# Feed-forward sums in PSUM banks, another ring placement, meta rows over four column groups, a second attention woven into projections

## What is computed

```python
h = [112 zero rows, 16 meta rows, 256 token rows]                 # first block
proj = rmsnorm(h) @ w_in                                           # q, k, v of 8 heads; q, f, i, g of 4 gated heads
h += concat(stick_breaking(sb_q, sb_k, sb_v), hgrn2(hg_q, hg_f, hg_i) * silu(hg_g)) @ w_out
h += hierarchical_moe(rmsnorm(h))                                  # 32 experts
x = rmsnorm(h[128:])
for layer in (0, 1):                                               # second block
    q, k, v, q_mem = projections of x                              # layer 1: "MoBA", 12 heads of 64, k and v from shared_w_kv
    mix = concat(attention(q, k, v), softmax(q_mem @ km.T / 8) @ vm) @ w_out
    x = layer_norm(ALPHA * x + mix)
    a, b = split(x @ ffn_w_in)                                     # two halves of 2816
    a = causal convolution of a over 3 tokens + bias
    x = layer_norm(ALPHA * x + (gelu(a) * b) @ ffn_w_out)
```

## Time and profile before

| | us |
|---|---|
| median of 3 runs | 1521.02 |
| the profiled execution | 1524.56 |
| its span, first to last instruction | 1522.8 |

### The profile page before, as it was taken

One profiled execution on the slowest core, in us unless ns is written; L12 is line 12 of the kernel. 1 busy time (PEld: TensorE's weight loads), 2 busy tenths in 40 slices (PEclk: granted clock), 3 DMA queues, 4 the chain that ended last, 5 costly groups with the idle time before them and its releaser, 6 DMA issues.

```text
span 1522.8 us, 18334 instructions
## 1 busy us (share of the span) xinstructions
PE 1270.6 (83%) x7464; PEld 821.1 (54%) x7464; DVE 601.2 (39%) x1127; ACT 263.7 (17%) x681; POOL 409.6 (27%) x379
## 2 busy tenths in 40 slices
PE   7999989776656667676998797999979978999995
PEld 6864554322212212122776557999437744999842
DVE  3432424101100000011105624988963052788986
ACT  4313431000000000001124611211001051111100
POOL 4000100000000000000002422988840032598881
PEclk9999889978878877778997899999999999999998
DMA  9613117999999999999633007844335512454300
GB/s 316 209 65 111 56 59 264 381 421 421 422 422 422 422 422 422 422 422 408 235 111 111 1 1 247 279 167 166 138 111 193 166 56 82 161 173 167 139 0 28
DMA packets 112758, 335.72 MB, mean 220 GB/s; under 512 B 6616, under 2 KB 58128, under 8 KB 88109
## 3 DMA queue, kind: packets, MB, share of 16 engines
q1 hardware_dynamic: 110070, 326.33, 56.3%
q0 software_dynamic: 2416, 8.30, 1.6%
q10 hardware_dynamic: 199, 0.06, 0.0%
HBM read 333.59 MB, written 2.86 MB: 221 GB/s over the span
## 4 chain that ended last, share of the span: by engine, by line
PE 62%; DMA 25%; DVE 8%; ACT 3%; issue 2%; SPq 1%; DVEq 0%; ACTq 0%
PE bank L767 23%; DMA ring<-in_w_expert_up 23%; PE bank L1441 18%; PE bank L1489 7%; PE bank L1087 5%; PE bank L1312 1%; DMA ring<-in_a_w_in 1%; PE bank L913 1%; DVE small L2484 1%; PE bank L1361 1%; ACT arena L1870 1%; SPq L664 1%; ACT arena L1879 1%; PE bank L1284 1%; DMA ring<-in_ffn_w_in 1%
## 5 line engine op out<-in xcount | busy, mean ns | idle before, releaser
L1087 PE MATMUL bank<-ring,arena 128*32 128x512 f32 x992 | 152.5, 771 | 122.1 <-DMA ring<-in_w_expert_up 109.6
L767 PE MATMUL bank<-ring,wide_rows 128*128 128x512 f32 (+3 forms) x416 | 172.2, 572 | 1.2 <-DVE wide_rows L2504 1.1
L1087 PEld LDWEIGHTS bank<-ring,arena 128*32 128x32 f32 x992 | 40.6, 137 | 232.8 <-issue 213.9
L767 PE MATMUL bank<-wide_rows,ring 128*128 128x256 f32 (+3 forms) x672 | 152.1, 383 | 4.9 <-DMA ring<-in_a_w_in 2.5
L767 PEld LDWEIGHTS bank<-wide_rows,ring 128*128 128x128 f32 (+1 forms) x672 | 128.0, 198 | 29.4 <-issue 9.3
L2318 DVE TENSOR_TENSOR arena<-arena,bank 64x512 f32<-64x512 f32 x16 | 11.1, 691 | 307.0 <-ACT arena L1764 307.0
L1441 PE MATMUL bank<-R,arena 128*128 128x128 f32 x1056 | 125.1, 275 | 0.0
L767 PEld LDWEIGHTS bank<-ring,wide_rows 128*128 128x128 f32 (+1 forms) x416 | 76.9, 188 | 86.6 <-issue 83.8
L1441 PEld LDWEIGHTS bank<-R,arena 128*128 128x128 f32 x1056 | 121.5, 192 | 0.0
L2772 POOL MEMSET arena<- 128x768 f32 (+2 forms) x3 | 1.1, 412 | 435.2 <-DVE X L2413 435.2
L1441 PE MATMUL bank<-wide_rows,ring 128*128 128x128 f32 x704 | 88.6, 282 | 12.7 <-DMA ring<-in_ffn_w_in 8.5
(11 more groups left out here) (364 smaller groups left out, 1851.8 us busy)
## 6 DMA issues: line engine op xcount, KB each, us to landing
ring<-in_w_expert_down SPq DMA_DIRECT2D x32, 2048.0 KB, 24.1
ring<-in_w_expert_gate SPq DMA_DIRECT2D x31, 2048.0 KB, 19.2
ring<-in_w_expert_up SPq DMA_DIRECT2D x31, 2048.0 KB, 23.7
ring<-in_ffn_w_in SPq DMA_DIRECT2D x44, 1024.0 KB, 8.3
ring<-in_ffn_w_out SPq DMA_DIRECT2D x10, 2048.0 KB, 7.8
ring<-in_w_in SPq DMA_DIRECT2D x7, 2048.0 KB, 15.4
ring<-in_shared_w_kv SPq DMA_DIRECT2D x3, 2048.0 KB, 7.8
ring<-in_w_out SPq DMA_DIRECT2D x2, 2048.0 KB, 10.5
```

Of the source, the lines that this page charges most:

```text
L767: last = pe.matmul(dst, lhsT, rhs, start=k == 0, stop=k == len(pairs) - 1)
L1087: last = pe.matmul(bank[e % 2][at:at + SLOTS, :], xg_tile(e % 2, k)[:, SLOTS * r:SLOTS * r + SLOTS], w[r][:, kk, :], start=k == 0, stop=k ...
```

## The change

**Meta rows.** The meta job now takes 32 stationary columns in place of 16 and sends its eight matmuls to four column groups of the array, two to each (L905); a new job (sbvs, hgis) adds the four partial results with one matmul by a 0/1 matrix by_slice, which GpSimd makes at the start. s0 moves from step 5 to step 6.

**Ring.** From feed-forward 0 on, the load order stays nearly the same (b_in 1 comes first of layer 1), but slots are given by SLOT_ORDER. Unit ffn_in 1 of layer 0 now goes to the slot of cmp_v, in place of that of the memory rows, and ffn_in 4 goes to the latter. b_out 1 goes to the slot of b_in 1, which is read until b_q 2.

**a_in.** Each of its three units is waited for where it is first read.

**Feed-forward.** summed writes its results to the bank y; the taps and the gate read them there; a tile's second bank is free again only after gate. down's products 1 to 7 go to other banks. GpSimd makes the sums of pairs 0 and 1 alone, hidden and weights; VectorE makes those of pairs 2 to 10 alone (pair_summed, in the order of SUM_ORDER). Product 5 of pair 0 waits until after product 6 of pair 1. The last three pairs wait for their sums one by one.

**Layer 1.** The list second_attention gives one order to TensorE and ScalarE, in which projections, attention steps and five eighths of each b_out job ("begun") stand alternately. Units begin with mem. In step i TensorE does scores(i), transposes(i - 2) and values(i - 3). Scores have banks 4 and 5, transposes bank 6 and values bank 7 alone, and so each waits for the unit before it. Outputs go to headT, in R. In feed-forward 1 tile 2's first quarters come ahead of the second token block as well.

The diff, cut to its core:

```diff
...
+SUM_ORDER = list(range(2, LAST_PAIRS[0])) + [STEPS_F - 1, STEPS_F - 3, STEPS_F - 2]
+SLOT_ORDER = (0, 3, 2, 5, 1, 4)
+LATE = 2
...
     ffn(0)
-    order += [("kv", c) for c in range(3)] + [("b_in", c) for c in range(2)] + [("b_out", c) for c in range(2)]
+    order += [("b_in", 1), ("kv", 0), ("b_in", 0), ("kv", 1), ("kv", 2)] + [("b_out", c) for c in range(2)]
     ffn(1)
...
+        placed[i // RING * RING + SLOT_ORDER[i % RING]] = key
...
+def second_attention():
+
+
+    return [("b_qm", 0), ("b_k", 0), ("step", 0), ("b_q", 0), ("step", 1), ("b_v", 0), ("step", 2), ("b_v", 1), ("step", 3), ("step", 4),
+            ("b_k", 1), ("step", 5), ("step", 6), ("b_q", 1), ("step", 7), ("step", 8), ("b_v", 2), ("step", 9), ("b_v", 3), ("step", 10),
+            ("b_k", 2), ("step", 11), ("b_q", 2), ("step", 12), ("begun", 0), ("step", 13), ("begun", 1), ("step", 14), ("begun", 2),
+            ("step", 15), ("begun", 3), ("step", 16), ("step", 17), ("step", 18)]
...
+                for k in range(2):
+                    for r in range(4):
+                        last = pe.matmul(b[SLOTS * r:SLOTS * (r + 1), :], XT[:, 4 * k + r, 0:SLOTS], w[:, 4 * k + r, :],
+                                         start=k == 0, stop=k == 1)
+                last.then_inc(job_done, 1)
+
+            def slices_summed(name, partial):
+                pe.wait_ge(slices_ready, 1)
+                b = to_fill(pe, name)
+                wait_emptied(pe, name[:-1], 2)
+                pe.matmul(b[0:META, :], by_slice[:, :], partial, start=True, stop=True).then_inc(job_done, 1)
...
+                if c not in wa:
+                    wa[c] = wait_weights(pe, ("a_in", c))[:, 0:KT * (A_CUTS[c + 1] - A_CUTS[c])].rearrange("p (k n) -> p k n", k=KT)
...
+                    if layer == 1:
+                        pe.wait_ge(at_tc, u)
...
                     if u >= 4:
                         pe.wait_ge(ph["summed"], u - 3)
                         first_columns(u, 0)
-                        first_columns(u, 1)
...
+                    if u >= 4:
+                        pe.wait_ge(ph["hidden"], u - 3)
+                        first_columns(u, 1)
...
+                    if p == 0:
+                        pe.wait_ge(ph["summed"], FFT - 1)
+                        pe.wait_ge(ph["hidden"], FFT - 3)
                     down(p, 1)
-                    down(p, 2)
-                    pe.wait_ge(ph["h_sums"], p + 1)
+                    pair_summed(p)
                     down(p, 3)
+                    down(p, 4)
+                    down(p, 7)
                     if p == 0:
                         pe.wait_ge(ph["summed"], FFT)
...
+                    if p == 1:
+                        pe.wait_ge(ph["hidden"], FFT - 1)
+                        down(0, 5).then_inc(ph["used"], 1)
+                    if p >= 1:
+                        down(p, 5).then_inc(ph["used"], 1)
...
-                pe.wait_ge(ph["h_sums"], STEPS_F)
-                pe.wait_ge(ph["x_sums"], 8)
                 for which in (1, 6, 5, 2, 3, 7, 4):
                     for p in LAST_PAIRS:
...
+                        if which == 6:
+                            pair_summed(p)
                         last = down(p, which)
...
+                    step(tt(r[:, P:2 * P], r[:, 0:P], x[:, P:2 * P], ALU.add))
+                    tt(twos(r[:, 2 * P:4 * P]), twos(x[:, 2 * P:4 * P]), r[:, P:2 * P].unsqueeze(1).broadcast_to([P, 2, P]), ALU.add)
+                    step(tt(y[:, 0:P], r[:, 0:P], y[:, 0:P], ALU.add))
+                    tt(y[:, 3 * P:4 * P], r[:, 3 * P:4 * P], x[:, 2 * P:3 * P], ALU.add)
+                    tt(y[:, P:3 * P], r[:, 2 * P:4 * P], y[:, P:3 * P], ALU.add).then_inc(ph["summed"], 1)
...
+                    weights_landed(dve, layer, "out", p // 2)
+                    dve.wait_ge(ph["used"], 4 if p == STEPS_F - 1 else p - 1)
                     dve.wait_ge(ph["hidden"], 2 * p + 2)
...
-                for p in range(STEPS_F - 1):
+                for p in range(2):
+                    hidden_summed(p)
+                for p in range(2):
                     down_summed(p)
...
```

More of the change, by code:

```diff
@@ L231, in plan_jobs @@
     add_normed("xTb")
-    j.add("b_k", "A", 3)
-    j.add("b_v", "A", 4)
-    j.add("b_q", "A", 3)
-    j.add("b_qm", "A", 1)
+    for what, i in second_attention():
+        if what[:2] == "b_":
+            j.add_part(what, i, "A")
     j.add("b_out", "V", 4)
@@ L244, in attention_units @@
     for layer in range(2):
+        main = []
         for pair in range(PAIRS):
@@ L746, in _ @@
                 load(second + u)
-            for n in range(first_unit["ffn0"], len(units)):
-                load(n)
+            for key in first_unit["late"]:
+                load(w_at[key])
             for tb in range(TB):
@@ L1440, in up_sums @@
                     for k in range(KT // 2):
-                        last = pe.matmul(up_banks[u % 4][i][:, at * P:(at + 1) * P], weights(k), columns(k), start=k == 0, stop=k == KT // 2 - 1)
+                        last = pe.matmul(up_banks[layer][u % 4][i][:, at * P:(at + 1) * P], weights(k), columns(k), start=k == 0, stop=k == KT // 2 - 1)
                     return last
@@ new lines, in mixed_ready, with b_out_part @@
+            def mixed_ready(k):
+                pe.wait_ge(at_oc, 8 + (k - PAIRS + 1 if k >= PAIRS else MEM_PAIRS + k + 1))
+            def b_out_part(job, ks):
+                tb, n = job // 2, job % 2
+                w = wait_weights(pe, ("b_out", n)).rearrange("p (k n) -> p k n", n=HALF)
+                b = to_fill(pe, "b_out", job) if ks[0] == b_first[0] else bank[jobs.bank("b_out", job)]
+                for k in ks:
+                    mixed_ready(k)
+                    last = pe.matmul(b[:, :], headT[:, k, tb * P:(tb + 1) * P], w[:, k, :], start=k == b_first[0], stop=k == b_last[-1])
+                return last
@@ L1576, in _ @@
+            b_first, b_last = (6, 7, 0, 1, 2), (3, 4, 5)
+            step = attend(1)
+            for what, i in second_attention():
+                if what == "step":
+                    step(i)
+                elif what == "begun":
+                    b_out_part(i, b_first)
+                else:
+                    project(what, i)
+            for job in range(4):
+                b_out_part(job, b_last).then_inc(job_done, 1)
             ffn(1, "xTf1", 6)
@@ L2697, in _ @@
             pool.memset(zeros[:, :], 0.0).then_inc(zero_ready, 1)
+            step(pool.memset(by_slice[:, :], 0.0))
+            for r in range(4):
+                last = pool.affine_select(out=by_slice[:, :], in_=by_slice[:, :], compare_op=ALU.not_equal, fill=1.0, base=-SLOTS * r,
+                                          pattern=[[-1, META]], channel_multiplier=1)
+                if r < 3:
+                    step(last)
+            last.then_inc(slices_ready, 1)
             step(pool.memset(tri[:, :], 1.0))
```

287 lines of the change are left out of this document (166 added, 121 removed).

## The result

| | before | after |
|---|---|---|
| median of 4 runs each, us | 1522.81 | 1486.95 |
| lowest to highest, us | 1520.92 to 1524.88 | 1484.72 to 1488.05 |
| the profiled execution, us | 1524.56 | 1488.05 |
| its span, us | 1522.8 | 1486.2 |

The ratio is 0.9762, with a 95% interval of 0.9741 to 0.9783: 35.9 us faster. Forecast were 1480 (range 1465 to 1492) and a gain of 40.8 us. Of the 7 us between the forecast and the median of 1486.95, 4.9 are gain that did not come, and 1.8 come from the median before, which was 1521.02 when the forecast was made and is 1522.81 over four runs.

A forecast was written before the change was run, and what follows sets the result against it. TensorE (62%) and the expert DMA stream (25%) bound the kernel; 7.7 + 2.5 + 9.8 + 14.0 + 6.8 = 40.8 us off the profiled 1524.6 gives 1483.8, median 1480, range 1465 to 1492.

The forecast's parts named there:

- Meta rows, 7.7: Two meta jobs on TensorE: 3.1 us each in place of 7.0, saving 7.7 us (between 6.5 and 8.5).
- The expert stream moves as a whole: Expert loads, 250 to 705 us: untouched, moved as a whole by what TensorE saves ahead of the router.
- a_in, 2.5: First query projection: its 2.54 us wait for the last of three units goes, saving 2.5 us, at worst 0.
- Start of feed-forward 0, 9.8: First quarters of tiles 2 and 3: load wait and low clock go, 8.1 + 1.7 = 9.8 us; 0.4 wait left.
- Tiles, 0: Feed-forward tiles: conv and gate read PSUM off the chain, the new wait for gate has slack; 0 us.
- Second products, 69.7 each: Both feed-forwards: 66.6 us of matmuls plus 3.1 of waits at pairs 0, 2 and 9; gain 14.0 us together.
- Layer 1, 131.0: Weaving projections with attention: 15.7 us less 8.9 of waits and changed form, gain 6.8; layer 1 in 131 us.
- The first and third: Rivals: GpSimd's hidden sums at 1.26 us each, 1493 (7%); ring change fails, ffn_in 1 held back, 1490 (4%).
- the second: Rival on layer 1: each of five waits followed by TensorE at 1.2 GHz, 1.7 to 2.9 us each, 1487 (12%).
- signs of being wrong: Profile after: VectorE sums above 1 us, 7 us at pair 0, single-step waits, gate waits, 1.2 GHz after short waits.
- The slower rival: Second products: VectorE becomes the bound at 12 us a pair, 66 us more twice, 1612 us (2%).

The follow-up runs named there:

- x_meta: Kernel after with both meta jobs again as eight matmuls of 16 columns and no joining job; median 1495.99 us, ratio 0.9824.
- i_best: Kernel after with halved layer 1 projections, own pair 2 buffers, step 12's scores last, hidden sums of pairs 0 and 1 on VectorE at tiles 8, 12; 1465.99 us.
- i_copy: Kernel after with ScalarE's copy of unit i - 2 ahead of the exponentials of unit i in layer 1; median 1480.41 us, ratio 0.9712.
- r_after: Kernel after, unchanged, measured again side by side with the best version; 1484.8 us, ratio 0.9746.
- i_three: Kernel after with own buffers for the sums of pair 2 in both second products; median 1478.2 us, ratio 0.9714.
- i_split: Kernel after with three layer 1 projections cut in halves, so a piece stands between attention steps up to step 12; median 1476.61 us, ratio 0.9708.
- i_all: Kernel after with halved layer 1 projections, own pair 2 buffers, GpSimd's pair 0 sums whole before pair 1's, step 12's scores last; median 1471.27 us, ratio 0.9646.

## Why the prediction was right, point by point

- **Meta rows, 7.7.** Mis-sized by little: 8.2 at full clock. The job takes 1.86 (forecast 1.84), the joining matmul 0.96 (0.87), and with what they add to their neighbours the two jobs come to 2.9 and 2.8 where 3.1 was put down: not every change of form has its 0.20.
- **The expert stream moves as a whole.** The loads did: the last weights for a gate and up product came 10.5 us earlier, the router 9.6. What failed is that nothing was put down for TensorE's own work behind them: 2.1 us stay behind, since its last gate and up product ran at the low clock, 6.46 us in place of 3.64. In other executions with the same code this stretch takes 466.1 to 469.6 us, 3.64 and 6.56 for that product among them, so nothing says that the change caused it.
- **a_in, 2.5.** The wait is gone, 2.7 in the table; undone it costs 1.7.
- **Start of feed-forward 0, 9.8.** 9.5, and 9.4 when undone. The wait that is left takes 0.68 (0.4 forecast).
- **Tiles, 0.** 130.4 in all kernels. VectorE's second tap and its gate fell from 1.38 and 1.34 us on average to 0.48 and 0.41, now with one operand in PSUM; TensorE had to wait for neither. GpSimd makes its sums beside them as before. The prediction said that the turn takes as long as before; it takes less, and no time comes of it.
- **Second products, 69.7 each.** Feed-forward 1 takes 70.0, with waits of 0.82, 1.99 and 0.27 for 0.6, 2.1 and 0.4. GpSimd's hidden sums take 0.45 to 0.46, as estimated, and VectorE's wide ones 0.69; a pair's eight sums take 3.5 us, not 3.84. Feed-forward 0 takes 71.6: the term that was missing is the low clock behind the wait at pair 2, 1.7 us. Of ten executions with this wait, five have it in feed-forward 0; in the other five that product takes 70.0.
- **Layer 1, 131.0.** 134.05, with two stretches of low clock of 1.6 behind waits. Without them 130.8. Its parts: the three waits 5.3 (4.9 forecast), the last copy 0.32 (0.4), the changed form 0.17 for each of 13 (0.20). Two steps were wrong, and cancel: b_out 1 was there in time (1.0 forecast; x_meta, with the same code there, waits 0.95, and i_best, which comes to it earlier, 0.52), and the scores of step 12 wait 0.69 us for the copy of b_q 2, which was not in the sum.
- **Rivals.** The first and third did not happen. Of the second, that each wait is followed by the low clock, the half happened: after two of three waits in layer 1 and one in feed-forward 0. The argument against it (a record of usual length behind 1.33 us) was drawn from a shorter wait: in i_copy waits up to 1.23 us were followed by none, those of 1.7 to 1.8 us in layer 1 by one 18 times in 24. It needed a price in the sum, 1.6 to 1.7 each. Two of the signs of being wrong that the prediction names did come up: this one, and a wait at a single step (12). The slower rival's mechanism is real, with 9.8 us a pair.

The sum missed by 4.2 us: meta +1.9, stream -2.1, feed-forward 0 -1.8, layer 1 -3.3, start of feed-forward 1 +1.6, the rest -0.5. But for 0.5 of meta work and the rest of -0.5, nearly all of this is clock. That the profiled sum is off by 4.2 only is in part luck: stretches of clock that help (meta, feed-forward 1) offset some that hurt, and another execution has others. Measured again (r_after), the kernel after was 39.8 us faster than the kernel before.

## What to carry to other kernels

Where TensorE is the bound, a short wait can have two prices: itself, and what follows at the low clock (18 of 24 times here, 1.6 to 1.7 us). Put a piece of independent work between any two dependent steps, even a halved one: that took 8.2 us from layer 1, where a longer lag took nothing away. Before a wait is charged to a lag, look at what stands ahead of the awaited instruction on its own engine, and at which chain comes second.

Give elementwise work with all its operands in SBUF to the engine that is alone at that time. The same sums on VectorE take 3.5 us a pair while GpSimd rests and 9.8 while it works.

## What the runs showed of the hardware

The same instructions take different times in different executions of one kernel, by the clock that TensorE is granted. Layer 0 from the first query projection to a_out, in the kernel after (first) and in the same kernel in a later execution (second); columns are the stretch, its length, busy time (and instructions) of TensorE, its weight loads, VectorE, ScalarE and GpSimd, the granted clock, the DMA share and GB/s:

```profile
725.50:873.26 147.76, 128.03 (x899) 98.43 (x897) 46.89 (x140) 54.87 (x174) 25.02 (x30) 0.90 0.30 100
```

```profile
724.50:867.26 142.76, 123.84 (x899) 94.59 (x897) 46.91 (x140) 54.74 (x174) 25.02 (x30) 0.93 0.33 110
```

Of the same stretches, two windows of 5 us that begin 110 us after the last experts' work, of the kernel after and of i_three:

```profile
818.30:823.30 5.00, 4.48 (x32) 3.33 (x32) 2.15 (x8) 2.66 (x11) 1.65 (x2) 0.55 0.18 56
```

```profile
817.80:822.80 5.00, 4.28 (x45) 3.17 (x46) 3.26 (x11) 2.93 (x13) 1.65 (x2) 1.00 0.11 34
```

Same counts in the long stretches, same busy time of the other engines, 5.0 us difference at a clock of 0.90 and 0.93. Over thirteen profiled executions, two of the kernel after and one of each of its eleven variants, this stretch took 141.0 to 147.8 us. It has waits of about 1 us throughout, and TensorE is at 1.2 GHz in different places of it: in the two windows above, the one runs 32 matmul records at 0.55 and the other 45 at 1.00. Four other stretches do the like: the experts (3.5 us), layer 1 (3.4), the start of feed-forward 1 (1.6) and the second product of feed-forward 0 (1.7). So the time of this kernel, with its many short waits, is uncertain by some us from this alone, and one execution can't tell an edit of 1 us from none: only the length of the stretch that was touched can. The profiled execution of i_best is such a case: with 147.8 us in layer 0 and 469.6 for the experts it took 1473.78 us, 7.8 above the median of its six runs. Why a wait of one length is followed by the low clock in one execution and not in the next stays open here. i_split, whose layer 1 has no such wait up to step 12, took 125.8 us there, i_all 125.45 and i_best 125.5, while the eight executions with the layer 1 of the kernel after went from 132.5 to 135.8.
